# Hybrid decoder step in fp32 on one core: first block with normed tiles from a scaled diagonal, plain tiles on ScalarE, one weight split ahead of a state update, and head variances in another bank

## What is computed

```python
h = _rmsnorm(x, ln_mix[0])                       # x * rsqrt(mean(x*x) + eps) * gain
proj = einsum('bld,de->ble', h, w_in)            # columns rq rk rv rg | mq mk mv mo | 8 gate columns
q, k = rope(rq), rope(rk); o_ret = silu(rg) * head_norm(retention(q, k, rv))
qk = silu(causal_conv(concat(mq, mk), carried rows))
h_m = head_norm(sigmoid(mo) * mlstm(q_m, k_m, mv, gates))
x = x + concat(o_ret, h_m) @ w_out
x = x + swiglu(rmsnorm(x))
```

## Time and profile before

| | |
|---|---|
| median of 3 runs | 1553.61 us (1551.95 to 1554.43) |
| the profiled execution | 1554.71 us |
| its span, first to last instruction | 1552.9 us |
| PE busy | 1502.3 us |
| DVE busy | 1172.6 us |
| ACT busy | 911.2 us |

### The profile page before, as it was taken

One profiled execution on the slowest core, in us unless ns is written; L12 is line 12 of the kernel. 1 busy time (PEld: TensorE's weight loads), 2 busy tenths in 40 slices (PEclk: granted clock), 3 DMA queues, 4 the chain that ended last, 5 costly groups with the idle time before them and its releaser, 6 DMA issues.

```text
span 1552.9 us, 23238 instructions
## 1 busy us (share of the span) xinstructions
PE 1502.3 (97%) x8623; PEld 1326.7 (85%) x8623; DVE 1172.6 (76%) x1290; ACT 911.2 (59%) x907; POOL 86.6 (6%) x92
## 2 busy tenths in 40 slices
PE   7999998999999989998999999999999999999997
PEld 5899788999999989987878888888888888888885
DVE  5756677545456797666688898988989888898886
ACT  4544535443334553333477777868778787777863
POOL 1023100000000000111110000000000000000002
PEclk9999999999999999999999999999999999999999
DMA  8577624996456423433599999999999999999993
GB/s 215 155 135 149 115 86 119 287 295 196 129 149 194 139 72 98 136 119 94 199 400 348 392 366 400 388 357 385 369 392 394 365 384 359 399 378 379 392 356 118
DMA packets 214583, 403.86 MB, mean 260 GB/s; under 512 B 14467, under 2 KB 131503, under 8 KB 214386
## 3 DMA queue, kind: packets, MB, share of 16 engines
q1 hardware_dynamic: 203104, 372.82, 69.1%
q0 software_dynamic: 6208, 22.06, 4.6%
q10 hardware_dynamic: 5202, 8.03, 1.5%
HBM read 372.58 MB, written 30.28 MB: 259 GB/s over the span
## 4 chain that ended last, share of the span: by engine, by line
PE 88%; DVE 8%; issue 1%; ACT 1%; DMA 1%; DVEq 0%; ACTq 0%; SPq 0%
PE bank L485 26%; PE bank L486 25%; PE bank L487 25%; PE bank L688 2%; DVE dense_lo L1726 1%; PE bank L942 1%; PE bank L1089 1%; PE bank L730 1%; PE bank L625 1%; ACT dense_hi L1293 1%; DVE w_lo L2261 1%; PE bank L680 1%; DMA arena<-in_x_sample 1%; PE bank L643 0%; DVE arena L2098 0%
## 5 line engine op out<-in xcount | busy, mean ns | idle before, releaser
L2261 DVE TENSOR_TENSOR w_lo<-arena,w_hi 128x2048 fp32r<-128x2048 f32 (+1 forms) x280 | 597.0, 2165 | 86.3 <-ACT w_hi L1605 85.0
L1605 ACT ACTIVATE w_hi<-arena 128x2048 fp32r<-128x2048 f32 (+1 forms) x280 | 500.6, 1819 | 114.4 <-PE bank L487 112.6
L485 PE MATMUL bank<-w_hi,xg_hi 128*128 128x512 f32 (+1 forms) x768 | 288.1, 375 | 2.8 <-DVE w_lo L2261 2.3
L486 PE MATMUL bank<-w_lo,xg_hi 128*128 128x512 f32 (+1 forms) x768 | 286.7, 373 | 0.0
L487 PE MATMUL bank<-w_hi,xg_lo 128*128 128x512 f32 (+1 forms) x768 | 285.9, 372 | 0.0
L1726 DVE TENSOR_TENSOR dense_lo<-ring,dense_hi 128x2048 fp32r<-128x2048 f32 (+1 forms) x78 | 169.2, 2170 | 121.6 <-ACT dense_hi L1293 121.5
L1293 ACT ACTIVATE dense_hi<-ring 128x2048 fp32r<-128x2048 f32 (+1 forms) x78 | 140.5, 1803 | 160.2 <-PE bank L487 134.3
L485 PE MATMUL bank<-h_hi,dense_hi 128*128 128x320 f32 x512 | 165.6, 324 | 17.2 <-DVE h_lo_o L1738 6.2
L485 PEld LDWEIGHTS bank<-w_hi,xg_hi 128*128 128x128 f32 x768 | 144.9, 189 | 32.0 <-issue 3.5
L487 PEld LDWEIGHTS bank<-w_hi,xg_lo 128*128 128x128 f32 x768 | 144.6, 188 | 26.0
L486 PEld LDWEIGHTS bank<-w_lo,xg_hi 128*128 128x128 f32 x768 | 144.9, 189 | 25.0
(11 more groups left out here) (420 smaller groups left out, 2328.0 us busy)
## 6 DMA issues: line engine op xcount, KB each, us to landing
arena<-in_w_moe_down SPq DMA_DIRECT2D x176, 512.0 KB, 6.5
arena<-in_w_moe_gate SPq DMA_DIRECT2D x128, 512.0 KB, 6.7
arena<-in_w_moe_up SPq DMA_DIRECT2D x128, 512.0 KB, 6.7
arena<-in_w_moe_gate SPq DMA_DIRECT2D x64, 384.0 KB, 5.4
arena<-in_w_moe_up SPq DMA_DIRECT2D x64, 384.0 KB, 3.9
ring<-in_w_in_ab SPq DMA_DIRECT2D x32, 512.0 KB, 9.0
ring<-in_w_in_c SPq DMA_DIRECT2D x32, 512.0 KB, 4.6
expert_rows<-ZERO SPq DMA_DIRECT2D x12, 1024.0 KB, 7.6
```

The lines of the kernel that those rows point to most:

```text
L485: mm(out, left[0], right[0], start=start, stop=False)
L486: mm(out, left[0], right[1], start=False, stop=False)
L1605: fn(WH[SLOT_OF[p]][:, 0:unit_size(p)], STAGE[:, s, 0:unit_size(p)], ACT.Copy).then_inc(S("unit_hi"), 1)
L2261: v.tensor_tensor(WL[w][:, 0:n], STAGE[:, s, 0:n], WH[w][:, 0:n].bitcast(F32), ALU.subtract).then_inc(S("unit_split"), 1)
```

## The change

- The scale of a token goes into a diagonal matrix (DIAG); a product of XN with it gives a normed tile in PSUM. ACT reads it with the gain as its scale and writes the high part, DVE multiplies and subtracts for the low part. Four such tiles are made before rq's first tile and four between its first half tile and the next. PE runs 18 products of zeros first.
- The plain tiles become steps x0 to x7, and the carried rows a step, after rq; ACT copies them out. All five come through the act ring.
- x is loaded in three pieces with a semaphore each. The gate columns and carried rows are loaded by POOL's queue, after unit 0 has landed, ahead of its other small loads.
- One `wl` moves from behind state4 to before mo1.
- The last variances and what follows use the tail rings. There ACT splits the next weight ahead of the parts of heads 6 and 7, and DVE makes the first three lower-bound operations after its split.

```diff
-    rq gates rk rope0 rope1 columns rv ...
+    rq x0 x1 x2 x3 carry gates x4 x5 x6 x7 rk rope0 rope1 columns rv ...
-    conv7 center1 silu7 wl mv4 score4 mv5 mo0 weigh4 wh shift5 mo1 state4 wl score5 wh center2 wl mo2
+    conv7 center1 silu7 wl mv4 score4 mv5 mo0 weigh4 wh shift5 wl mo1 state4 score5 wh center2 wl mo2
@@ PE, group_tiles
-                            if ready and j == 0:
-                                pe.wait_ge(S(ready), k + 1)
+                            if first and j == 0:
+                                after_empty(pe, ("n0", k))
...
+                        elif first and j == 0:
+                            first_tiles(range(KD // 2, KD))
@@ PE, start
+            pe.wait_ge(S("zero"), 3)
+            for n in range(WARM):
+                if n == WARM - 3:
+                    pe.wait_ge(S("const_in"), 16)
                     pe.wait_ge(S("prm_in"), 16 * 8)
...
+                mm(banks[3][:, 0:256], ZERO[:, 0:P], ZERO[:, :], start=True, stop=True)
+            pe.wait_ge(S("token_scales"), 3)
+            def first_tiles(ks):
+                for k in ks:
+                    b = open_bank("dve")
+                    for i, (t0, tn) in enumerate(BLK):
+                        ins = mm(b[:, t0:t0 + tn], XN[:, i, k * P:(k + 1) * P], DIAG[:, i, 0:tn], start=True, stop=True)
+                    close_bank("dve", ins, ("n0", k))
+            first_tiles(range(KD // 2))
+            def residual_tile(k):
+                b = open_bank("act")
+                for i, (t0, tn) in enumerate(BLK):
+                    ins = nc.tensor.transpose(b[:, t0:t0 + P], XN[:, i, k * P:(k + 1) * P], ident)
+                close_bank("act", ins, ("xT", k))
@@ PE, end of the mixer
+            part.update(act="tail_act", dve="tail_dve")
             head_variances("hn0", 1)
...
-            part.update(act="tail_act", dve="tail_dve")
@@ ACT
-            fn(V1[:, :], ZERO[:, 0:3], ACT.Square)
-            act.wait_ge(S("x_in"), 32)
+            fn(V1[:, :], ZERO[:, 0:3], ACT.Sqrt)
             for i, (t0, tn) in enumerate(BLK):
+                act.wait_ge(S(f"x_in_{i}"), 16)
...
+            def first_high(k):
+                after_fill(act, ("n0", k))
+                after_empty(act, "prm")
+                b = bank_of(*ticket[("n0", k)])
+                fn(HH[:, k, :], b[:, 0:NT], ACT.Copy, scale=prow("ln_mix", k)).then_inc(S("n0_hi"), 1)
             split_dense()
-            high("n0", OR)
+            for k in range(KD // 2):
+                first_high(k)
             split_dense()
+            for k in range(KD // 2, KD):
+                first_high(k)
...
+                elif name == "x":
+                    free(fn(xT[:, u, :], take(("xT", u))[:, 0:NT], ACT.Copy))
...
             head_roots("hn0", 1)
+            split_dense()
             for u in HEADS[1]:
                 after_empty(act, ("hn0", "scale", u))
                 mixed_high("mix0", OR, u)
-            split_dense()
@@ DVE
+            v.memset(XN[SMP:P, 2, :], 0.0)
+            step(v.memset(DIAG[:, 2, :], 0.0))
+            dve.wait_ge(S("token_roots"), 1)
+            step(v.reciprocal(RS[:, :], RS[:, :]))
+            for i, (t0, tn) in enumerate(BLK):
+                v.tensor_scalar(DIAG[0:tn, i, 0:tn], ident[0:tn, 0:tn], RS[0:tn, i:i + 1], None, ALU.mult).then_inc(
+                    S("token_scales"), 1)
             split_dense()
             after_empty(dve, "prm")
+            for k in range(KD):
+                dve.wait_ge(S("n0_hi"), k + 1)
+                free(v.scalar_tensor_tensor(out=HL_A[:, k, :], in0=take(("n0", k))[:, 0:NT], scalar=prow("ln_mix", k),
+                                            in1=HH[:, k, :].bitcast(F32), op0=ALU.mult, op1=ALU.subtract))
+                if k == KD // 2 - 1:
+                    split_dense()
@@ POOL
+            pool.wait_ge(dense_landed[0], 32)
+            pool.dma_start(wgate[:, :, :], w_ab[:, :, 4096:4104]).then_inc(S("wgate_in"), 16)
+            pool.dma_start(CN[0:24, :], A["state_conv"][0].rearrange("b j c -> (b j) c")).then_inc(S("carry_in"), 16)
+            pool.dma_start(NN[0:32, :], A["state_mlstm_n"][0].rearrange("b h k -> (b h) k")).then_inc(S("carry_in"), 16)
```

More of the change, by code:

```diff
@@ L252, in trunk_kernel @@
         OH = region(0, KD, NT)
-        XN = region(0, 3, D)
+        XN = region(5120, 3, D)
+        DIAG = region(1024, 3, P)
         PN = region(3072, P)
@@ L354, in trunk_kernel @@
         FETCH = sb("FETCH", [P, 2])
+        WARM = 18
         ZERO = sb("ZERO", [P, 256])
@@ L542, in half_used, with group_tiles @@
                 unit_read[place[key]] = (S("half_used"), h + 1)
-            def group_tiles(src, c, ready):
+            def group_tiles(src, c, first):
                 for half in range(2):
@@ L649, in _, with carried @@
                     close_bank("act", ins, "prm")
[L650 to L660, removed]
+                mm(banks[3][:, 0:256], ZERO[:, 0:P], ZERO[:, :], start=True, stop=True)
[12 more added lines that the diff above has]
+                close_bank("act", ins, ("xT", k))
+            def carried():
+                pe.wait_ge(S("carry_in"), 32)
+                b = open_bank("act")
+                for k in range(KD):
+                    nc.tensor.transpose(b[:, 24 * k:24 * k + 24], CN[0:24, k * P:(k + 1) * P], ident[0:24, 0:24])
+                ins = nc.tensor.transpose(b[:, 192:224], NN[0:32, :], ident[0:32, 0:32])
+                close_bank("act", ins, "carry")
             HA = (HH, HL_A)
@@ L789, in _ @@
                 if name in ("rq", "rk"):
-                    group_tiles(HA, GROUP[name], "n0_h" if name == "rq" else None)
+                    group_tiles(HA, GROUP[name], name == "rq")
                 elif name == "rv":
@@ L809, in _ @@
                     token_block(need_unit(*key), HA, key, ("V", 0, 1), u % 3)
+                elif name == "x":
+                    residual_tile(u)
+                elif name == "carry":
+                    carried()
                 elif name == "gates":
@@ L1144, in _ @@
             x_s = A["x_sample"].rearrange("b t d -> (b t) d")
-            sp.dma_start(XN[:, 0:2, :], x_p).then_inc(S("x_in"), 16)
-            sp.dma_start(XN[0:SMP, 2, :], x_s).then_inc(S("x_in"), 16)
+            for i in range(2):
+                sp.dma_start(XN[:, i:i + 1, :], x_p[:, i:i + 1, :]).then_inc(S(f"x_in_{i}"), 16)
+            sp.dma_start(XN[0:SMP, 2, :], x_s).then_inc(S("x_in_2"), 16)
             def load_dense(n):
@@ L1455, in _ @@
                     split_dense()
+                elif name == "x":
+                    free(fn(xT[:, u, :], take(("xT", u))[:, 0:NT], ACT.Copy))
+                elif name == "carry":
+                    b = take("carry")
+                    act.wait_ge(S("history_zero"), 1)
+                    fn(CARRY.rearrange("p k n -> p (k n)"), b[:, 0:192], ACT.Copy)
+                    free(fn(NS0, b[:, 192:224], ACT.Copy))
                 elif name == "gates":
@@ L1764, in _ @@
             v.memset(RS[:, :], 1.0).then_inc(S("scales_one"), 1)
[L1765 to L1769, removed]
+            v.memset(XN[SMP:P, 2, :], 0.0)
[5 more added lines that the diff above has]
+                    S("token_scales"), 1)
             split_dense()
             after_empty(dve, "prm")
-            after_empty(dve, ("xT", KD - 1))
-            scale = take("n0_scale")
-            for k in range(KD + 1):
-                if k < KD:
-                    ins = v.scalar_tensor_tensor(out=OR[:, k, :], in0=xT[:, k, :], scalar=prow("ln_mix", k),
-                                                 in1=scale[:, 0:NT], op0=ALU.mult, op1=ALU.mult)
-                    ins.then_inc(S("n0_value"), 1)
-                    if k == KD - 1:
-                        dve.wait_ge(S("n0_value"), KD)
-                if k > 0:
-                    low("n0", k - 1, OR, HL_A)
-            free(v.memset(RS[:, :], 1.0))
-            split_dense()
+            for k in range(KD):
+                dve.wait_ge(S("n0_hi"), k + 1)
[3 more added lines that the diff above has]
+                    split_dense()
             def group_values(c):
@@ L2007, in projected_out @@
                 scale_of(tag)
-            bound = prm[:, PRM["hg_lower"]:PRM["hg_lower"] + 16].rearrange("p (a b) -> p a b", b=8)
-            step(v.tensor_tensor(LBT[:, 2, :], bound[:, 0, :], bound[:, 1, :], ALU.max))
-            v.tensor_tensor(LBT[:, 0, :], bound[:, 0, :], LBT[:, 2, :], ALU.subtract)
-            v.tensor_tensor(LBT[:, 1, :], bound[:, 1, :], LBT[:, 2, :], ALU.subtract).then_inc(S("lb_max"), 1)
             head_reciprocals("hn0", 1)
@@ L2018, in _ @@
             split_dense()
+            bound = prm[:, PRM["hg_lower"]:PRM["hg_lower"] + 16].rearrange("p (a b) -> p a b", b=8)
+            step(v.tensor_tensor(LBT[:, 2, :], bound[:, 0, :], bound[:, 1, :], ALU.max))
+            v.tensor_tensor(LBT[:, 0, :], bound[:, 0, :], LBT[:, 2, :], ALU.subtract)
```

(1 more changed line is left out.)

19 lines of the change are left out of this document (2 added, 17 removed).

## The result

The changed kernel takes 1559.87 us (median of 5 runs, 1559.19 to 1562.21), the kernel before beside it 1553.24 us (5 runs, 1551.95 to 1554.43). The ratio is 1.0048, 95% interval 1.0036 to 1.0059: slower by 0.48%, 6.6 us between the medians, where 0.24% and 3.7 us were forecast. The profiled execution took 1559.51 us, its span 1557.7, so 4.8 us above the profiled one of before.

A forecast was written before the change was run, and what follows sets the result against it. TensorE (PE), 88% of the chain that ended last, was taken to bound the kernel. Head +13.3, low half -2.5 and variances -7.1 summed to +3.7 us: 1557.3 us against the median of 1553.61, range 1549.5 to 1563.

The forecast's parts named there:

- the head: Changed first block: 13.3 us late at rk's end, a distance that what follows keeps.
- Head to the first product: Start of the first block: rq's first product at 16.4 us instead of 21.08.
- Four normed tiles inside: Between rq's first half tile and the next: four more normed tiles cost PE 2.2 us.
- Between rq and rk: Plain tiles, carried rows and gates after rq: ACT's copy at 35.0, 1.6 us clock loss, gates end at 41.6.
- The bank of plain tile 4: rk's first tile needs x4's bank, copied after ACT's gate rows: PE stands 42.8 to 52.0, rk 10.8 us late.
- Restart at the low level: rk after the stop starts at the low clock: 2.5 us lost, between 1.7 and 3.4.
- The low half ahead of state4: At mo, PE's idle 2.51 us until 166.42 goes, PE continuing at 163.9: -2.5 us.
- Variances in another bank: Output projection: starts at 223.6 without the bank wait, clock stays high, second weight starts at 235.0; together -7.1 us.
- (a): Clock also low when rq starts, slowing k steps and tiles inside: 1561 to 1564 us; chance 0.13.
- (b): ACT frees x4's bank earlier, so rk starts at 42.8, 1.6 late: -8.0, 1545.6 us; chance 0.08.
- (c): Clock stays high through the plain tiles and rises soon in rk: +1.3, 1554.9 us, no change; chance 0.25.
- (d): Tail does not pay; low parts or reciprocal end last, only idle 2.4 us goes: 1562.0 us; chance 0.06.

The follow-up runs named there:

- the reordered kernel: The changed kernel with plain tiles 4 to 7 ahead of the gate products instead of behind them; 1546.93 us, ratio 0.9967.
- the end of the mixer alone: The kernel before with only the variances in the other bank, the split ahead of the mixed high halves and the lower-bound softmax behind; 1543.80 us, ratio 0.9954.
- the new head at its best place: The changed kernel in the order rq, carried rows, gate products, rk, plain tiles 0 to 7; 1542.66 us, ratio 0.9935.
- all three reorderings: The changed kernel with plain tiles behind rk, wide tables' DMA behind unit 3's split, state loads behind unit 6's landing; 1543.27 us, ratio 0.9926.
- the head alone: The changed kernel with the low half back behind state4 and the end of the mixer as before; 1571.27 us, ratio 1.0119.
- both good parts: The kernel before with the changed end of the mixer and the low half ahead of state4, head untouched; 1543.24 us, ratio 0.9949.

## Why the prediction was right, point by point

The direction, the mechanism and two of three terms were right; the third, the head, was too small by 2.1 us at the second score, and the whole by 2.8. The forecast of 0.24% lies outside the measured interval (0.36 to 0.59), and two smaller misses hid part of the head's: unit 0 landed 0.9 us earlier than taken, and the restart cost 0.4 less. That the sum of the traces (+6.5) and the difference of the medians (6.6) meet so closely is in part luck, since the profiled pair ends at 4.8.

1. *Head to the first product.* 16.4 forecast, 15.44 measured. Unit 0 landed at 10.6, earlier than the 11.5 taken.
2. *Four normed tiles inside.* 2.2 us forecast, 2.59 measured (17.27 to 19.86). The Trainium skill, "TensorE: Matmul & The Clock Gate", Terms, would have made it 4.8; a plain tile, transposed, takes 0.33 us (the nine transposes at 44.10 start 0.109 us apart) where a normed one takes 0.65, so the ratio here is 2 and not 4.
3. *Between rq and rk: the step that failed in size.* The prediction let ACT split unit 3 at rq's end (35.0), saying that the loads "have more time than they need". They don't: the tables' load, issued at 20.20, took until 34.23, unit 3 until 34.94. That is 2.3 us (tile 3 at 37.26 for 35.0), and the run with that load moved gives it back. The stay at 1.2 GHz, taken as 3.4 us from the earlier trace rows, was 6.8 (35.5 to 42.3), but much of it lay over the idle: from tile 3 to the last gate product 6.84 us went by where 6.6 were forecast (24 products in 4.92 for 5.1, tile 3 and the carried rows in 1.92 for 1.4). Gates ended at 44.1 for 41.6.
4. *The bank of plain tile 4.* Right in cause and size: 8.95 us idle, gate rows of 10.0, rk at gates' end plus 10.8. Three orders of the same steps put the stop ahead of rk's first tile, ahead of its second, or nowhere, as counted.
5. *Restart at the low level.* 2.5 forecast between 1.7 and 3.4; 2.1 measured against the order without a stop.
6. *The low half ahead of state4.* -2.5 forecast; the wait is gone, 0.3 us of waiting for DVE's reciprocal (L1937) came back at 187.66, -2.2 in all. The traces show it; its own timing is too coarse to say more than between -4 and +2 us.
7. *Variances in another bank.* -7.1 forecast, -7.0 from 220 to 244 us in the changed kernel and in the end of the mixer alone, as in all ten traces that have it (6.9 to 7.0); timed alone -0.46% (-7.1 us, between -4.8 and -9.6). Right in its parts too: the idle, the clock and the second weight.

Of the rivals, (a), a low clock at rq, did not occur, and in the execution with 3 warming matmuls it did not either; (b), that ACT frees the bank early, is what the reordered kernel does on purpose, at 1546.9 where (b) was priced at 1545.6; (c) was wrong about the head and (d) about the tail. "More than they need" was said of loads for whose landing the prediction shows no row; that sentence is where the 2 us went.

What stays open: at the end of the first layer the changed kernel is 6.5 us behind, in the profiled executions as a whole 4.8. The 1.7 in between come from waits and clock stays between 540 and 820 us that differ in every trace, and no run isolates them. In the pair for the end of the mixer alone 4.1 us of its 11.5 lie there too.

## What to carry to other kernels

When steps are reordered on one engine, number the tiles of each accumulator ring in the old and in the new order and write beside each the engine, and the place in that engine's order, that empties it; a short tile put behind a long job of the emptying engine holds the ring for the whole job. A large move whose sum is small should be split: here +1.19%, -0.46% and about -0.1% were hidden in one +0.48%. The kernel with the new head at its best place (0.9935) can't be told from the one with the old head and the other two parts (0.9949, the intervals overlap). And before a load is called hidden, read its landing and what else is on the DMA engines then.

## What the runs showed of the hardware

**A load's price is that of its company.** One unit's second piece took 15.6 us to land beside the tables' load and 9.0 without it; unit 6's second piece took 12.8 and 15.8 us beside three state loads in two executions, 7.9 when these waited. With both loads moved (all three reorderings) the same two pieces took 9.2 and 9.4.

**A stretch of transposes and idling does not always cost clock.** In the changed kernel PE only transposed or idled from 32.27 to 39.18, and 0.50 was granted from 35.5 on. With 3 warming matmuls the same stretch lasted from 33.89 to 38.19 with 2.0 us idle, and with the tiles behind rk from 50.63 to 55.1 with 1.5 us idle, both at 1.00:

```profile
33.89:38.19 4.30, 2.29 (x23) 1.84 (x20) 1.49 (x1) 3.43 (x6) 0.00 (x0) 1.00 0.61 235
```

```profile
50.60:55.10 4.50, 3.00 (x27) 2.59 (x25) 4.04 (x2) 4.50 (x11) 2.32 (x3) 1.00 0.26 55
```

The Trainium skill, "TensorE: Matmul & The Clock Gate", Part 4, says that transposes don't count as busy for the clock. The long stretch agrees, though 3.84 us of it were idle; in the two short ones no price was paid. What decides between them is not shown.

**The price of a stop in clock varies.** The stop of 2.51 us ahead of mo's second tile pair was followed by a clock of 1.00 in the kernel before (166.42 on) and by 3.4 us at 0.50 in the head alone (181.91 to 185.32). The stop of 1.01 us in the run with the state loads moved was followed by 10.2 us at 0.50.

**Slower executions are those with more time at the low level.** The kernel with both good parts took 1539.46 us at a mean granted clock of 0.995 and 1552.83 at 0.983. Over 155 timed executions of this study, each taken against the mean of its own kernel in its session, a microsecond more at 1.2 GHz goes with 0.33 us more time (correlation 0.79, worked out from span and mean clock, which has three digits). A wait costs time itself and can be followed by the low level, so this does not say which of the two comes first. A single profiled pair can thus differ by several microseconds in stretches that nobody changed. From 540 to 820 us the distance of the changed kernel shrinks from +6.5 to +4.9; the granted clock there, first before, then after:

```profile
540.00:820.00 280.00, 262.69 (x1723) 234.94 (x1722) 208.96 (x380) 126.50 (x152) 32.12 (x27) 0.94 0.47 163
```

```profile
540.00:820.00 280.00, 257.39 (x1745) 231.35 (x1745) 210.66 (x387) 124.85 (x152) 32.79 (x27) 0.96 0.46 156
```
